# Streaming float32r weight columns in interleaved, descending 64-byte runs

## What is computed

```python
x = x + 0.5 * swiglu_ffn(rms_norm(x, ffn1_norm_g), ffn1_w_gate, ffn1_w_up, ffn1_w_down)   # 2048 -> 5632 -> 2048
u = rms_norm(x, mix_norm_g) @ w_in                     # 2048 -> 4096 + 768 + 512 + 64 + 2048 + 2048
y_conv = conformer_conv_branch(u_conv, ...)            # 31 taps, layer norm, silu, @ (2048 x 2048)
y_mla = mla_branch(c_q_raw, c_kv_raw, k_rope_raw, ...) # 16 heads, 128 + 64 wide, @ (2048 x 2048)
x = x + (sigmoid(gl_conv) * y_conv + sigmoid(gl_mla) * y_mla) @ w_out
x = x + 0.5 * swiglu_ffn(rms_norm(x, ffn2_norm_g), ffn2_w_gate, ffn2_w_up, ffn2_w_down)
return rms_norm(x, final_norm_g)
```

## Time and profile before

| | |
|---|---|
| median of 3 runs | 2327.43 us (2326.33 to 2327.43) |
| profiled execution | 2326.71 us |
| its span, first to last instruction | 2324.8 us |
| mean granted TensorE clock | 0.998 |
| TensorE busy | 2299.0 us (99%), 10718 matmul records |
| VectorE busy | 1322.2 us (57%) |
| ScalarE busy | 1188.3 us (51%) |
| DMA queue of the weights | 430.93 MB, 60.0% of 16 engines |

### The profile page before, as it was taken

How to read it: one execution, slowest core, us unless ns; L and a number is a source line. 1 busy time by engine, 2 the same in 40 slices (tenths; PEclk the granted TensorE clock), 3 DMA queues, 4 the chain that set the end, 5 groups by cost and what they waited for, 6 DMA issues and landing times.

```text
span 2324.8 us, 26788 instructions
## 1 busy us (share of the span) xinstructions
PE 2299.0 (99%) x10718; PEld 1924.4 (83%) x10718; DVE 1322.2 (57%) x1470; ACT 1188.3 (51%) x1620; POOL 0.2 (0%) x4
## 2 busy tenths in 40 slices
PE   8999999999999999999999999999999999999997
PEld 7888888888888888878889888888888888888886
DVE  5544544544545488997875465555544544544443
ACT  6444444444444577787776564444444444444443
POOL 0000000000000000000000000000000000000000
PEclk9999999999999999999999999999999999999999
DMA  8666666666665665566643455656666666666664
GB/s 289 189 190 190 190 185 196 190 187 192 190 191 187 186 199 183 171 198 182 199 136 119 138 174 185 189 184 208 188 186 196 191 186 189 191 188 193 195 191 135
DMA packets 121532, 432.65 MB, mean 186 GB/s; under 512 B 13632, under 2 KB 13888, under 8 KB 121280
## 3 DMA queue, kind: packets, MB, share of 16 engines
q1 hardware_dynamic: 121408, 430.93, 60.0%
HBM read 428.78 MB, written 2.10 MB: 185 GB/s over the span
## 4 chain that ended last, share of the span: by engine, by line
PE 97%; DVE 1%; ACT 1%; issue 1%; DMA 0%; SPq 0%; ACTq 0%; DVEq 0%
PE bank L682 31%; PE bank L684 31%; PE bank L683 31%; PE turned L693 2%; PE bank L825 1%; PE bank L799 1%; PE bank L800 1%; DVE q_rope L1117 0%; PE turned L810 0%; ACT w_hi L432 0%; DVE w_lo L927 0%; DVE q_rope L1123 0%; DMA raw<-in_ffn_up 0%; PE turned L879 0%; ACT q_rope L540 0%
## 5 line engine op out<-in xcount | busy, mean ns | idle before, releaser
L927 DVE TENSOR_TENSOR w_lo<-raw,w_hi 128x1024 fp32r<-128x1024 f32 (+2 forms) x814 | 986.9, 1215 | 954.8 <-ACT w_hi L432 954.5
L432 ACT ACTIVATE w_hi<-raw 128x1024 fp32r<-128x1024 f32 (+2 forms) x814 | 853.0, 1051 | 998.4 <-PE bank L684 987.9
L682 PE MATMUL bank<-w_hi,h 128*128 128x512 f32 (+1 forms) x2144 | 835.9, 390 | 10.1 <-DVE w_lo L927 10.1
L684 PE MATMUL bank<-w_hi,h 128*128 128x512 f32 (+1 forms) x2144 | 832.7, 388 | 0.0
L683 PE MATMUL bank<-w_lo,h 128*128 128x512 f32 (+1 forms) x2144 | 832.6, 388 | 0.0
L682 PEld LDWEIGHTS bank<-w_hi,h 128*128 128x128 f32 x2144 | 403.0, 188 | 92.7 <-DVE w_lo L927 11.4
L684 PEld LDWEIGHTS bank<-w_hi,h 128*128 128x128 f32 x2144 | 402.9, 188 | 83.1
L683 PEld LDWEIGHTS bank<-w_lo,h 128*128 128x128 f32 x2144 | 403.1, 188 | 81.6
L682 PE MATMUL bank<-w_hi,hidden 128*128 128x512 f32 x704 | 274.3, 390 | 0.0
L684 PE MATMUL bank<-w_hi,hidden 128*128 128x512 f32 x704 | 273.9, 389 | 0.0
L683 PE MATMUL bank<-w_lo,hidden 128*128 128x512 f32 x704 | 273.9, 389 | 0.0
(11 more groups left out here) (171 smaller groups left out, 1223.4 us busy)
## 6 DMA issues: line engine op xcount, KB each, us to landing
raw<-in_ffn_up SPq DMA_DIRECT2D x352, 512.0 KB, 4.1
raw<-in_ffn_down SPq DMA_DIRECT2D x176, 512.0 KB, 3.6
raw<-in_conv_in SPq DMA_DIRECT2D x64, 512.0 KB, 3.8
raw<-in_conv_gate SPq DMA_DIRECT2D x32, 512.0 KB, 4.2
raw<-in_mla_gate SPq DMA_DIRECT2D x32, 512.0 KB, 4.2
raw<-in_mla_out SPq DMA_DIRECT2D x32, 512.0 KB, 3.6
raw<-in_conv_out SPq DMA_DIRECT2D x32, 512.0 KB, 3.7
raw<-in_w_out SPq DMA_DIRECT2D x32, 512.0 KB, 3.6
```

What stands on the lines that cost most here:

```text
L432: act.activation(w_hi[:, j, 0:n], raw[:, j, 0:n], ACT.Copy).then_inc(hi_ready, 1)
L682: pe.matmul(dst, fixed_hi, moving_hi, start=first, stop=False)
L684: return pe.matmul(dst, fixed_lo, moving_hi, start=False, stop=last)
L927: dve.tensor_tensor(w_lo[:, j, 0:n], raw[:, j, 0:n], w_hi[:, j, 0:n], ALU.subtract).then_inc(lo_ready, 1)
```

## The change

`w_hi` and `w_lo` hold each block of `w` columns in another order. The host cuts the columns into runs of 16 (64 bytes), puts the even runs into the first half of the block and the odd runs into the second half, and each half's runs in reverse. In `wide_unit` the moving operand becomes a pattern of three dimensions that reads them back in the order of the output columns: the last run of the first half, the last run of the second half, the last but one of the first half, and so on. For 512 columns these are 32 runs; two that follow each other are 1024 bytes apart, the next pair lies 64 bytes lower. PSUM receives the same columns in the same order as before. Loads, rounding and splitting still treat the unit as contiguous. `head_units`, `head_pair` and all other matmuls are as before. An unused tensor of 64 bytes behind `w_lo` moves `x`, `h` and everything after them by 64 bytes, while `raw`, `w_hi` and `w_lo` stay where they are.

```diff
+RUN = 16
 UNIT = WIDE * DEEP
...
         w_lo = sb("w_lo", [P, SLOTS, UNIT], F32R)
+
+        sb("after_weights", [P, 16])
         x = sb("x", [P, 2, D])
...
+            def in_turns(block):
+
+                return block.rearrange("p (h n t) -> p n h t", h=2, t=RUN)[:, ::-1, :, :]
+
             def wide_unit(u, g):
...
-                    moving = w_hi[:, slot, r * w:(r + 1) * w], w_lo[:, slot, r * w:(r + 1) * w]
+                    moving = in_turns(w_hi[:, slot, r * w:(r + 1) * w]), in_turns(w_lo[:, slot, r * w:(r + 1) * w])
...
 def units_of(w):
     k, width = w.shape
+    w = w.reshape(k, width // (2 * RUN), 2, RUN)[:, ::-1].transpose(0, 2, 1, 3)
     return w.reshape(k // (DEEP * P), DEEP, P, width).transpose(0, 2, 1, 3).reshape(-1, P, DEEP * width)
```

## The result

The changed kernel takes 2330.22 us (median of 20 runs, 2327.87 to 2335.28) against 2327.12 us before (20 runs, 2326.28 to 2327.76). The ratio is 1.0015 (95% interval 1.0008 to 1.0022): a little slower, inside the 0.2% that the forecast called no change. The 93 us forecast did not come.

What follows compares the result with a forecast made beforehand. TensorE's matmul count times spacing was taken to bound the kernel; 9384 wide matmuls gaining 10.7 ns gave 100.4 us, less 6.9 taken back, 93.5 us, so 2326.7 became 2233 us; 8-in-10 range 2222 to 2350 us.

Steps and rivals of the forecast that it cites:

- What bounds the kernel: Whole kernel: TensorE busy 99% of the span, so time is 9384 wide matmuls times their 226.7 ns spacing.
- surcharge over 216 ns: Wide matmuls: 10.7 ns of each 226.7 ns spacing could go, 9384 x 10.7 = 100 us.
- taken back: Start and 900 to 1085 us: DMA feed and VectorE limits return 2.4, 2.2 and 2.3 us of the gain.
- What the 13.3 ns are: Wide matmuls: time beyond 512 columns' 213.3 ns comes from weight load and full-rate moving read interfering in SBUF by address.
- slower* rival: Wide units, lines 682 to 684: moving read restarts at 31 joints per matmul; 2332 to 2450 us, chance 0.22.
- half-rate rows: Profile rows of float32 value multiplications and transposes, moving operand read at half rate, only 2.6 and 2.1 ns beyond their columns.
- term of 10.7 ns a matmul: Wide matmuls: spacing falls from 226.7 to 216.0 ns on 9384 matmuls, 100 us before deductions.
- rival *nothing: Wide matmuls: surcharge belongs to the float32r weight swap, or interleaving isn't at 64 bytes; 2327 us, chance 0.12.
- heads' matmuls: Head stage, 672 matmuls of 256 columns: only the 64-byte shift touches them; -7.2 to +8.9 us, taken as 0.

Runs made afterwards that it cites:

- still stream: Kernel before, but the moving operand of a wide unit reads its first column over and over (step 0): 2232.00 us against 2327.11.

## Why the forecast was wrong, step by step

**What bounds the kernel** was right. TensorE's spacing is the time: every kernel above moves by about its change in spacing times 9384. Also right was what the surcharge over 216 ns is worth, though only kernels that don't compute the products showed it. The still stream gives 2327.11 - 2232.00 = 95.1 us; 9384 x (226.9 - 216.3) ns = 99.5 us, so 4.4 us are taken back, where the forecast had 6.9. In that trace the wide matmuls wait 12.9 us in all for w_lo, against 10.1 us before (about 8 us of both at the start), which is 2.8 us of it.

**What the 13.3 ns are** was half right. That the spacing hangs on the relation of two address sequences is shown four ways: by the shift alone, the order alone, the reversal and the period of 256 bytes. The guesses that the order must go down and that 64 bytes then help were right in sign: within the new order the reversal is worth 12.5 ns and the shift 5.0 ns. What wasn't shown is that avoiding a meeting brings the surcharge of 13.3 ns down to 2.6. Here the measurement differs from the rule of the Trainium skill, "SBUF — State Buffer", section "Who interferes with whom", by which TensorE never waits and its two read ports are independent: at full rate 64 bytes of shift are worth 6.4 ns on each matmul. That page's section "Door 1: The DMA port swizzle" lets 64-byte joints go free. The runs don't contradict it and don't show it: 31 joints and none both stand at 226.67 ns, and since the still stream without joints has 216.3, a joint costs at most 10.4 / 31 = 0.33 ns in the changed kernel. The *slower* rival's price of a clock a joint, 0.42 ns, is above that bound, though its 2448 us is about what the ascending order costs.

**The step that failed** is the price: "I take 216.0, because a pattern that doesn't collide is what the half-rate rows are." The forecast reasoned as if the order and the shift were added to a kernel that collides, and as if not lying on top of each other were all that is needed. The runs say otherwise. Contiguous columns with no shift were already the best of the contiguous versions tried (13.5 ns against 20.0 and 19.1 ns), and the new order with its shift is the best of the ones in turns and downwards among runs of 16 read upwards (14.2 against 15.0 to 19.1 ns). The change goes from one good relation to another about as good, over two bad ones. No walking order came below 13.3 ns in the mean, so the term of 10.7 ns a matmul, 100 us in the sum, measured -0.6 ns: 226.9 to 227.5. The rival *nothing* came true, at 0.12, but not for its reasons: the surcharge isn't a fixed price of the swap, and SBUF does tell 64-byte places apart.

**Where the forecast could have seen it.** The half-rate rows show streams with half the fetches, not streams that avoid the load. And all stationary buffers of the kernel before lie at the same remainder modulo 2048 as w_hi; the rows gave 226.7 ns in every long stretch for all of them, so there was no row of a worse relation in the wide stage to say what that one was already worth.

**Smaller terms.** The heads' matmuls were put at 0 between -7.2 and +8.9 us; they gave about -2 us. The group of 320 columns, where the halves are 640 bytes apart and so not the same place, went from 146.6 to 149.9 ns, 0.3 us more; the forecast had counted it among the rest. It doesn't follow the others in all: with the shift alone it stayed at 146.6 ns.

**What stays open** is the rest of 10.7 ns. It isn't proportional to the length of the load, doesn't go when the load stands still, and doesn't go with any tried order, but goes with a still stream. Whether it is the fetching itself or a meeting that these orders can't avoid was not settled, and no kernel ran the stream without weight loads. One rival stands: in the changed kernel the meetings may be gone and 31 joints of up to 0.33 ns each take their place. No run has this order without its joints. That before and after both have exactly 226.67 ns speaks against it, since two different causes would have to agree to the digit, but the grid described at the end can make different needs come out at one spacing. Shifts finer than 64 bytes were not tried.

## What to carry over

When two operands are read at full rate side by side, treat their placement and the order of reading as one choice: here each half of the change cost 50 to 60 us and both together 3 us, so a trial of either alone would have misled in either direction. Before pricing such a change at a floor, measure the floor and the present state with a stream that stands still; it takes one line and says how much there is to win, though not that any real order wins it. And ask of a steady spacing whether it is a best case already: a kernel whose buffers all share one remainder may be sitting in it.

## What the runs showed that was not expected

The matmuls start on a grid. In the long stretches the spacings average 226.67, 230.00, 233.33 or 240.00 ns and, for 256 columns, 113.3 and 120.0 (single ones can differ: with the shift alone 231 and 236 ns follow each other). These are multiples of 6.67 ns, or of half of it, and the slow pattern of four adds up to 947 ns, 142 times 6.67. Worked out over the start times in nanoseconds, all settled stretches of one trace have the same remainder modulo 6.67 ns to within 0.2 ns, apart from an even drift of 1.6 parts in a million, through all the waits between them and in the kernel before and the changed one alike. After a wait the spacing of one matmul seems to depend on where in the 6.67 ns it starts (before, from 224 to 240 ns), and a stretch wanders until it finds a point that repeats. That fits a surcharge that looks like a constant in the kernel before, and a change that leaves no trace in most groups and yet tips a whole group into another pattern, as in the five slow stretches. With the still stream no such grid shows: its matmuls are 215 or 216 ns apart, with about every sixth at 220. What beats at 6.67 ns, the time of 16 columns, no row says.
